# Input projection: sums of squares as rows of four heads side by side, then short products to columns

## The chip, the cores and the metric

The kernel runs on one core of a Trainium2 chip. The metric is the device time of one launch in microseconds (us), taken as the median of several runs; less is better. Here TensorE (PE) multiplies matrices out of SBUF into PSUM, VectorE (DVE) and ScalarE (ACT) do elementwise work and empty PSUM, GpSimd (POOL) and SyncE (SP) carry the rest and the DMA queues. The engines run side by side and meet only at semaphores: an engine that waits on one holds up everything queued behind the wait.

## The reference, cut to what matters

One inference step of two layers over 640 tokens (512 latent, 128 context) of width 1024. Each layer projects its normed input once to all that its three attention branches need. The branch that this change touches is the gated delta net: queries and keys (four heads of 128 features each) go through a short convolution and SiLU, and are then divided by their own length, token by token and head by head:

```python
qkv = _short_conv(dn_qkv, lp['dn_conv_w'])          # 3 taps, then silu
def _l2norm(x):
    xf = x.astype(jnp.float32)
    return xf * lax.rsqrt(jnp.sum(xf * xf, axis=-1, keepdims=True) + EPS)
qn = _l2norm(q) * (DN_DK ** -0.5)
kn = _l2norm(k)
```

So a sum of 128 squares is wanted for each of 640 tokens, 4 heads, and keys and queries: 8 vectors of 640 sums in each of 2 layers.

## The kernel before

**Layout.** Activations lie feature-major: 128 features on the partitions, tokens in the columns. A token's sum of squares is therefore a sum over partitions, which TensorE makes.

**The projection.** `wstat` makes one output tile of 128 features x 640 tokens in PSUM banks 0 to 3 (two banks for each of two tiles in turn). It runs over 8 blocks k of the inner dimension; at each k it issues six matmuls (three products of split numbers, two halves of 320 tokens), 48 in a tile. `for j in range(PT_)` with PT_ = 24 runs 24 such tiles in each layer. Tile 0 holds gates, tiles 1 to 4 the keys (i = 0 to 3), tiles 5 to 8 the queries (i = 4 to 7), tiles 9 to 12 the values, later tiles the inputs of the other branches.

**The other engines** have their own loops over j, each one step behind. At step j DVE (`scaled(j - 1)`, L1737 and L1738) empties tile j-1, at even j splits the next weights (`split_lo`, L1505, after ACT's `split_hi`, L952), and runs the convolution of tile j-2 (`taps`, L1786 and L1789); ACT at step j casts weights (even j), writes tile j-1 out with its bias (`tile_out`, L1154, and the middle tap L1159), and makes SiLU and squares of an earlier tile (`conv_silu(j - 3)`, L1165 and L1170 into `SQT`). In layer 0 alone DVE also makes modulation rows (`mod_tile`, L1765) at steps 2 to 12, and PE, at j = 1 to 9, small products (`ada`, L469, and `adt`, L476) that wait for DVE's copy `ada_row` (L1778) of the previous one.

**The sums of squares.** After tile j (j = 4 to 11) PE waits for the squares of i = j - 4 and multiplies five blocks of 128 tokens of `SQT` (as the stationary operand) by one column of ones (L2442), which gives 5 columns of bank 7. ACT takes roots of the keys' twenty columns at j = 8 (L1197) and of the queries' twenty at j = 12 (L1205); DVE inverts them (L1878, L1833). Eight times a layer PE then spreads a head's inverse lengths over partitions into the bank pair 4 and 5, `pair(2)` (L2462; j = 8 to 11 keys, 13 to 16 queries), and DVE multiplies the head by them (`unit`, L1799, at its steps 9 to 12 and 14 to 17). `unit` counts `chat` up by two. From j = 9 to 12 PE also multiplies unit keys with themselves (L2452, `kdm`), which waits for `chat`.

**After the projection** PE turns values and keys by token and goes on to attention, the delta net's solves, the output projection and the MLP.

Of the kernel before, what the change touches and what calls it, by code (L numbers as in the profile page):

```python
# [7 lines left out]
F32 = mybir.dt.float32  # L8
# [5 lines left out]
P = 128  # L14
# [10 lines left out]
H = 4  # L25
# [82 lines left out]
def rotations():  # L108
# [15 lines left out]
PER = dict(  # L124
    w_mm=TILES, w_ev=TILES, par_in=32, tab_in=16 * 7, s0_in=32, st=64, std=32,
    h_hi=2 * KT, h_lo=2 * KT, h_sh=2, h_sl=2,
    pads=3, p_out=PT_, tap=12, taps=12, conv=12, silu=12, csq=8, css=8, crt=2, crr=2, kdm=4, kde=4, kdw=272, gce=2, gcr=144, mke=1, mex=1, wi=2, leaf=1, wst=320, crb=8, chat=16,
    msq=3, mss=1, mrt=2, mrr=1, mrb=2, map_=3, vtr=4, vte=4, ktr=4, kte=4,
    g_tr=1, g_cp=1, gate_e=2, gate_b=4, gate_mm=1, gate_t=3, gate_x=6,
    ga=96, gb=64, dtm=10, dta=10, eg=8, de=10, dtn=10, ke=8, qe=8, qs=8, kk=9, cm=10, atm=10, u1=20, pm=10, pe_=10,  # L130
# [19 lines left out]
def build(nc, t):  # L150

    ctx = ExitStack()
    with ctx:
# [41 lines left out]
        TSV = place("TSV", [P, T], F32, r_t + 25600)  # L195
        TGK = place("TGK", [P, T], F32, r_t + 28160)
        FLO = place("FLO", [P, H, T], F32R, r_t + 10240)
        SQT = [place(f"SQT{i}", [P, 641], F32, r_t + 10240 + i * 2592) for i in range(2)]
        UUD = [place(f"UUD{d}", [P, H, NB, LEAF], F32, r_t + (17920, 28160)[d]) for d in range(2)]
        UTD = [place(f"UTD{d}", [P, H, NB, LEAF], F32, r_raw + KT * CH * 4 + d * NM * LEAF * 4) for d in range(2)]  # L200
        KDR = place("KDR", [P, LEAF, LEAF], F32, r_x)
# [113 lines left out]
        def bank(i):  # L315
            return PS[:, i, :]
# [42 lines left out]
        def toks(b):  # L359
            return slice(b * P, (b + 1) * P)  # L360
# [12 lines left out]
        def conv_at(i):  # L373

            return (i + 4) % 8 if i < 8 else i
# [123 lines left out]
        with nc.Block() as block:  # L499
# [447 lines left out]
            def _(act):  # L947
# [188 lines left out]
                for l in range(DEPTH):  # L1136
# [25 lines left out]
                    def conv_silu(i):  # L1162

                        act.wait_ge(S["conv"], o["conv"] + i + 1)
                        nc.scalar.activation(QKV[:, conv_at(i), 1:642], TC[i % 2][:, 0:641], ACT.Silu).then_inc(S["silu"], 1)  # L1165
                        if i < 8:
                            act.wait_ge(S["silu"], o["silu"] + i + 1)
                            if i >= 2:
                                act.wait_ge(S["css"], o["css"] + i - 1)
                            nc.scalar.activation(SQT[i % 2][:, :], QKV[:, conv_at(i), 1:642], ACT.Square).then_inc(S["csq"], 1)  # L1170


                    for j in range(PT_ + 1):
# [6 lines left out]
                        if j == 1:  # L1180
                            root(2 * l)
                        if j == CKV0 + 1:
                            act.wait_ge(S["css"], o["css"] + 8)
                        if j == Z0 + 1 and l == 0:
                            act.wait_ge(S["ada_mm"], 8)
                        if j >= 1:
                            tile_out(j - 1)
                        if l == 0 and j == 1:
                            act.wait_ge(vb_in, 16)
                            nc.scalar.activation(CBX[:, :, :], CBX[:, :, :], ACT.Silu).then_inc(silu_c, 1)  # L1190
                        if 0 <= j - 3 < 12:
                            conv_silu(j - 3)
                        if j == 8:
                            act.wait_ge(S["css"], o["css"] + 4)
                            act.wait_ge(S["gce"], o["gce"] + 2)
                            act.wait_ge(S["gate_t"], o["gate_t"] + 2)
                            nc.scalar.activation(SMALL[:, 7, 0:20], bank(7)[:, 464:484], ACT.Sqrt, bias=eps).then_inc(S["crt"], 1)  # L1197
                        if 10 <= j <= 13:
                            h = j - 10
                            act.wait_ge(S["kdm"], o["kdm"] + h + 1)  # L1200
                            nc.scalar.copy(KD[:, h * NB:(h + 1) * NB, :],
                                           bank(7)[:, 208:368].rearrange("p (b c) -> p b c", b=NB)).then_inc(S["kde"], 1)
                        if j == 12:
                            act.wait_ge(S["css"], o["css"] + 8)
                            nc.scalar.activation(SMALL[:, 7, 20:40], bank(7)[:, 484:504], ACT.Sqrt, bias=peps,  # L1205
                                                 scale=float(P)).then_inc(S["crt"], 1)
                        if j == 14:
                            act.wait_ge(S["mke"], o["mke"] + 1)
                            nc.scalar.activation(LM[leafs, :, :, :], LM[leafs, :, :, :], ACT.Exp).then_inc(S["mex"], 1)
# [281 lines left out]
            def _(dve):  # L1491
# [278 lines left out]
                for l in range(DEPTH):  # L1770
# [40 lines left out]
                    for j in range(PT_ + 1):  # L1811
# [17 lines left out]
                        if 9 <= j <= 12:  # L1829
                            unit(j - 9)  # L1830
                        if j == 13:
                            dve.wait_ge(S["crt"], o["crt"] + 2)
# [33 lines left out]
                        if j == 8:  # L1866
                            dve.wait_ge(S["gate_mm"], o["gate_mm"] + 1)
                            for x in (0, 32):
                                nc.vector.tensor_copy(GCT[x:x + NM, :, :],
                                                      bank(7)[x:x + NM, 208:464].rearrange("p (d c) -> p d c", d=2)  # L1870
                                                      ).then_inc(S["gce"], 1)
                            nc.vector.tensor_copy(R[3], bank(7)[:, 128:168]).then_inc(S["gate_t"], 1)
                            nc.vector.tensor_copy(R[4], bank(7)[:, 168:208]).then_inc(S["gate_t"], 1)
                            dve.wait_ge(S["gate_t"], o["gate_t"] + 2)
                            link(nc.vector.tensor_scalar(R[8], R[3], -1.0, None, ALU.mult))
                            nc.vector.tensor_tensor(R[12], R[4], R[3], ALU.subtract).then_inc(S["gate_t"], 1)
                            dve.wait_ge(S["crt"], o["crt"] + 1)
# [407 lines left out]
            @block.tensor  # L2285
            def _(pe):

                def wstat(tile, g, mh, ml, n, lo, c, norm=None, tail=None, ks=range(KT)):

                    s, u = g % 2, tile % 2  # L2290
                    if u == 0:
                        pe.wait_ge(lo_ready, g + 1)
                    if tile >= 2:
                        pe.wait_ge(S["w_ev"], tile - 1)
                    for k in ks:
                        pe.wait_ge(lo, c + k + 1)
                        if k == 5 and norm is not None:
                            norm_turn(norm)
                        cols = slice(k * CH + u * P, k * CH + (u + 1) * P)
                        mlk = tail[:, k - H, :] if tail is not None and k >= H else ml[:, k, :]  # L2300
# [98 lines left out]
                for l in range(DEPTH):  # L2399
# [9 lines left out]
                    def adt(j):  # L2409

                        pe.wait_ge(S["ada_ev"], j + 1)
                        ada_turn(pe, MODB[j % 2], j).then_inc(S["ada_tr"], 1)

                    pe.wait_ge(S["h_sl"], 2 * l + 1)
                    for j in range(PT_):
                        wstat(t0 + j, g0 + j // 2, HH, HL, W1, S["h_lo"], 16 * l, 2 * l if j == 1 else None)
                        if j == 0:
                            norm_sums(2 * l)
                        if j == 3:
# [7 lines left out]
                        if j == 8:  # L2427
                            pe.wait_ge(S["gate_t"], o["gate_t"] + 2)
                            pe.wait_ge(S["gce"], o["gce"] + 2)
                            pe.wait_ge(S["crt"], o["crt"] + 1)  # L2430
                        if 10 <= j <= 13:
                            pe.wait_ge(S["kde"], o["kde"] + j - 9)
                        if j == 12:
                            pe.wait_ge(S["crt"], o["crt"] + 2)
                        if l == 0 and 2 <= j <= 9:
                            adt(j - 2)
                        if 4 <= j <= 11:
                            i = j - 4
                            pe.wait_ge(S["csq"], o["csq"] + i + 1)
                            for b in range(NB):  # L2440
                                c = cblk(b)
                                last = pe.matmul(bank(7)[:, 464 + i * NB + b:465 + i * NB + b],  # L2442
                                                 SQT[i % 2][:, c.start - 1:c.stop - 1], one, start=True, stop=True)
                            last.then_inc(S["css"], 1)
                        if 9 <= j <= 12:
                            h = j - 9
                            pe.wait_ge(S["chat"], o["chat"] + 2 * h + 2)
                            for b in range(NB):
                                for q in range(NQ):
# [558 lines left out]
```

## Time and profile before

| | before |
|---|---|
| median of 3 runs | 1824.38 us (1823.56 to 1825.29) |
| the profiled execution | 1822.96 us, of which the span from first to last instruction is 1821.2 us |
| PE busy | 1745.0 us (96%) |
| DVE busy | 1266.6 us (70%) |
| ACT busy | 847.3 us (47%) |
| mean granted TensorE clock | 0.983 of full |

The page gives busy times, 40 slices of the span with the granted clock, the chain of work that ended last followed back from the end, and the costliest groups of instructions. In all rows, times are us from the start of the span. A float32 matmul stands as two records, so 5 matmuls are x10. The name in front of an arrow is the tile written, the names behind it are those read.

### The profile page before, as it was taken

How to read it: one execution, taken by the hardware profiler on the slowest of the kernel's cores; microseconds unless marked ns; L12 is line 12 of the kernel's file. 1: busy time of each engine (PE TensorE's matmuls, PEld its weight loads, DVE VectorE, ACT ScalarE, POOL GpSimd, SP SyncE). 2: the span in 40 equal slices, each digit the busy share in tenths (PEclk: the TensorE clock that was granted, in tenths of full speed). 3: DMA queues.
4: the chain of work that ended last, by engine and by line, in shares of the span. 5: the costliest groups of instructions: out<-in, count | busy, mean ns of one | idle time of the engine just before them, and what ended most of it. 6: DMA issues, size and time to landing. Idle time of an engine off the chain costs nothing.

```text
span 1821.2 us, 33568 instructions
## 1 busy us (share of the span) xinstructions
PE 1745.0 (96%) x13554; PEld 1658.5 (91%) x13554; DVE 1266.6 (70%) x2117; ACT 847.3 (47%) x1469; POOL 523.9 (29%) x418
## 2 busy tenths in 40 slices
PE   5999999999999999999999999998999999999997
PEld 2889986788999999999999999777899999989997
DVE  2687775687735677676764557666977777788886
ACT  1555426744242231322325653475446666666664
POOL 5000002085442150321551000213832233232225
PEclk9999999989999999999999999998999999999998
DMA  8653223022467879688527761541132777877662
GB/s 344 252 207 93 78 73 68 1 66 88 165 226 218 282 234 325 244 268 275 193 91 204 181 154 47 139 94 42 49 107 85 222 234 249 298 277 256 214 221 91
DMA packets 128037, 316.66 MB, mean 174 GB/s; under 512 B 37828, under 2 KB 64236, under 8 KB 108172
## 3 DMA queue, kind: packets, MB, share of 16 engines
q1 hardware_dynamic: 121740, 279.49, 43.7%
q0 software_dynamic: 4608, 33.56, 9.5%
q8 instruction: 108, 1.77, 0.4%
q10 hardware_dynamic: 1536, 1.48, 0.2%
q14 instruction: 45, 0.37, 0.1%
HBM read 286.01 MB, written 95.49 MB: 209 GB/s over the span
## 4 chain that ended last, share of the span: by engine, by line
PE 82%; DVE 8%; issue 3%; DMA 3%; ACT 3%; SPq 1%; POOL 0%; POOLq 0%; ACTq 0%; DVEq 0%
PE PS L2305 47%; PE PS L2374 18%; PE PS L2668 1%; DMA ADA<-ada 1%; PE PS L2579 1%; PE PS L2757 1%; PE PS L2774 1%; PE PS L2628 1%; PE PS L2607 1%; PE PS L2596 1%; PE PS L2744 1%; DVE WHL L1559 1%; DVE MPR L1765 1%; PE PS L2442 1%; PE PS L2616 1%
## 5 line engine op out<-in xcount | busy, mean ns | idle before, releaser
L2305 PE MATMUL PS<-HH,HI 128*128 128x320 f32 (+1 forms) x1280 | 300.5, 316 | 5.2 <-DVE HL L1514 5.2
L2305 PE MATMUL PS<-HL,HI 128*128 128x320 f32 (+1 forms) x1280 | 295.9, 313 | 0.0
L2305 PE MATMUL PS<-HH,LO 128*128 128x320 f32 (+1 forms) x1280 | 294.5, 311 | 0.0
L952 ACT CAST HI<-RAW 128x2048 fp32r<-128x2048 f32 x64 | 121.9, 1905 | 276.6 <-PE PS L2305 249.4
L2305 PEld LDWEIGHTS PS<-HH,HI 128*128 128x128 f32 x1280 | 216.1, 191 | 5.8 <-issue 5.7
L2305 PEld LDWEIGHTS PS<-HL,HI 128*128 128x128 f32 x1280 | 219.7, 192 | 0.0
L2305 PEld LDWEIGHTS PS<-HH,LO 128*128 128x128 f32 x1280 | 217.7, 191 | 0.0
L2374 PE MATMUL PS<-FB,WHL 128*128 128x320 f32 x1344 | 199.6, 309 | 5.9 <-DVE TMP L1642 3.0
L2374 PEld LDWEIGHTS PS<-FB,WHL 128*128 128x128 f32 x1344 | 197.1, 188 | 8.2 <-DVE WHL L1559 6.2
L2374 PE MATMUL PS<-HB,WHL 128*128 128x322 f32 (+1 forms) x1344 | 200.0, 311 | 3.5 <-issue 1.6
L2374 PEld LDWEIGHTS PS<-HB,WHL 128*128 128x128 f32 x1344 | 199.0, 189 | 4.2 <-issue 2.5
L999 ACT CAST WHL<-RAWB 128x512 fp32r<-128x512 f32 x224 | 137.7, 619 | 111.9 <-PE PS L2374 93.1
L1505 DVE TENSOR_TENSOR LO<-RAW,HI 128x2048 fp32r<-128x2048 f32 x62 | 149.0, 2403 | 57.7 <-ACT HI L952 57.4
L2305 PE MATMUL PS<-FH,HI 128*128 128x320 f32 x768 | 175.5, 310 | 1.6 <-issue 1.6
L1559 DVE TENSOR_TENSOR WHL<-RAWB,WHL 128x512 fp32r<-128x512 f32 x224 | 168.9, 779 | 10.2 <-ACT WHL L999 8.6
L2305 PE MATMUL PS<-FH,LO 128*128 128x320 f32 x768 | 174.6, 308 | 0.0
L1765 DVE SCALAR_TENSOR_TENSOR MPR<-WM,CB 128x1024 f32<-128x1024 f32 x96 | 137.9, 1436 | 12.5 <-DMA WM<-adt 10.9
L2305 PE MATMUL PS<-FL,HI 128*128 128x320 f32 x640 | 145.9, 309 | 0.0
L2305 PEld LDWEIGHTS PS<-FH,HI 128*128 128x128 f32 x768 | 127.8, 188 | 2.0 <-issue 1.1
L2305 PEld LDWEIGHTS PS<-FH,LO 128*128 128x128 f32 x768 | 128.4, 188 | 0.0
L2305 PEld LDWEIGHTS PS<-FL,HI 128*128 128x128 f32 x640 | 107.0, 188 | 0.0
L928 POOL TENSOR_TENSOR TC<-TC 128x640 f32<-128x640 f32 x32 | 50.4, 1575 | 181.4 <-ACT FH L1450 181.4
(355 smaller groups left out, 2909.8 us busy)
## 6 DMA issues: line engine op xcount, KB each, us to landing
RAW<-ws SPq DMA_DIRECT2D x64, 1024.0 KB, 5.0
wp<-ws SPq DMA_DIRECT2D x32, 1024.0 KB, 7.9
RAWB<-wp SPq DMA_DIRECT2D x128, 256.0 KB, 3.9
WM<-adt SPq DMA_DIRECT2D x48, 512.0 KB, 9.1
RAWB<-ws SPq DMA_DIRECT2D x96, 256.0 KB, 3.7
FS<-hb SPq DMA_DIRECT2D x28, 640.0 KB, 7.9
ADA<-ada SPq DMA_DIRECT2D x16, 1024.0 KB, 7.6
wp<-ws POOLq DMA_DIRECT2D x16, 1024.0 KB, 10.2
```

The lines of the kernel that those rows point to most:

```text
L928: nc.gpsimd.tensor_tensor(TC[u][:, 0:T], TC[u][:, 0:T], TC[u][:, 0:T], ALU.mult).then_inc(S["f1_sq"], 1)
L952: nc.scalar.copy(HI[g % 2][:, :], RAW[g % 2][:, :]).then_inc(hi_ready, 1)
L999: nc.scalar.copy(WHL[:, w % SLOTS, 0, :], operand(w)).then_inc(F["whi"], 1)
L1505: last = nc.vector.tensor_tensor(LO[g % 2][:, c], RAW[g % 2][:, c], HI[g % 2][:, c].bitcast(F32), ALU.subtract)
L1559: nc.vector.tensor_tensor(WHL[:, w % SLOTS, 1, :], operand(w), WHL[:, w % SLOTS, 0, :].bitcast(F32), ALU.subtract).then_inc(F["wlo"], 1)
L1765: return nc.vector.scalar_tensor_tensor(out=MPR[:, :], in0=w[:, :], scalar=1.0, in1=cond[:, g, :], op0=ALU.mult, op1=ALU.mult, accum_out=M ...
L2305: last = pe.matmul(bank(2 * u + a)[:, 0:e], w[:, cols], m[:, a * HT:a * HT + e], start=(k == 0 and f), stop=(k == KT - 1 and e_))
L2374: last = pe.matmul(out, x[:, cols], B[:, y, k, 0:n], start=(opens and k == 0 and v == 0), stop=(k == H - 1 and v == 2), skip_group_check=n ...
L2442: last = pe.matmul(bank(7)[:, 464 + i * NB + b:465 + i * NB + b], SQT[i % 2][:, c.start - 1:c.stop - 1], one, start=True, stop=True)
L2579: pe.matmul(pair(0)[:, 0:LAT], q, kt[:, 0:LAT], start=True, stop=True)
L2596: last = pe.matmul(bank(7 if i else 2)[:, c:c + hi - lo], TSQ[rows, p, toks(b)], KSW[rows, lo:hi], start=True, stop=True)
L2607: last = pe.transpose(pair(2)[:, toks(i)], TC[a % 2][:, toks(slot)], ident)
```

## The change

PE no longer makes eight groups of five one-column products a layer. Keys and queries are taken four heads at a time. `square_rows(n)` (n = 0 keys, 1 queries) multiplies 32 columns of ones (stationary) by the squares of a head (moving, 512 and then 128 tokens), for four heads into partitions 0, 32, 64 and 96 of `pair(2)`. ACT copies the 128 x 640 result to a new tile `SQR`. `square_sums(n)` then multiplies the five token blocks of `SQR` (stationary) by four columns of the identity, which puts the same twenty sums into bank 7. `square_rows(0)` stands inside tile 7, before its block k = 2, and `square_rows(1)` at the same place of tile 12; `square_sums` follow after tiles 7 and 12. `SQT` has four buffers where it had two. The queries' root on ACT moves from step 12 to 13.

```diff
-        SQT = [place(f"SQT{i}", [P, 641], F32, r_t + 10240 + i * 2592) for i in range(2)]
+        SQT = [place(f"SQT{i}", [P, 641], F32, r_t + 8192 + i * 2592) for i in range(H)]
+        SQR = place("SQR", [P, T], F32, r_t + 24576)
...
-                            if i >= 2:
-                                act.wait_ge(S["css"], o["css"] + i - 1)
+                            if i >= H:
+                                act.wait_ge(S["css"], o["css"] + 1)
...
                         if j >= 1:
                             tile_out(j - 1)
+                        if j in (7, 12):
+                            act.wait_ge(S["css"], o["css"] + (1 if j == 7 else 3))
+                            nc.scalar.copy(SQR[:, :], pair(2)).then_inc(S["crt"], 1)
...
+                        if j == 13:
+                            act.wait_ge(S["css"], o["css"] + 4)
+                            nc.scalar.activation(SMALL[:, 7, 20:40], bank(7)[:, 484:504], ACT.Sqrt, bias=peps,
+                                                 scale=float(P)).then_inc(S["crt"], 1)
...
-                        if j == 12:
-                            act.wait_ge(S["css"], o["css"] + 8)
-                            nc.scalar.activation(SMALL[:, 7, 20:40], bank(7)[:, 484:504], ACT.Sqrt, bias=peps,
-                                                 scale=float(P)).then_inc(S["crt"], 1)
...
+                        if k == 2 and between is not None:
+                            between()
...
+                    def square_rows(n):
+                        pe.wait_ge(S["csq"], o["csq"] + 4 * n + 4)
+                        if n:
+                            pe.wait_ge(S["chat"], o["chat"] + 8)
+                        else:
+                            pe.wait_ge(S["g_cp"], o["g_cp"] + 1)
+                        for src, dst in ((slice(0, LAT), slice(0, LAT)), (slice(C_CTX - 1, C_CTX - 1 + CTX), slice(LAT, T))):
+                            for i in range(H):
+                                last = pe.matmul(pair(2)[32 * i:32 * i + 32, dst], ones[:, 0:32], SQT[i][:, src],
+                                                 start=True, stop=True)
+                        last.then_inc(S["css"], 1)
+
+                    def square_sums(n):
+                        pe.wait_ge(S["crt"], o["crt"] + 2 * n + 1)
+                        for b in range(NB):
+                            c = 464 + 20 * n + b
+                            last = pe.matmul(bank(7)[:, c:c + 3 * NB + 1:NB], SQR[:, toks(b)], ident[:, 0:P:32],
+                                             start=True, stop=True)
+                        last.then_inc(S["css"], 1)
...
-                        wstat(t0 + j, g0 + j // 2, HH, HL, W1, S["h_lo"], 16 * l, 2 * l if j == 1 else None)
+                        wstat(t0 + j, g0 + j // 2, HH, HL, W1, S["h_lo"], 16 * l, 2 * l if j == 1 else None,
+                              between=(lambda: square_rows(j // 12)) if j in (7, 12) else None)
...
-                        if 4 <= j <= 11:
-                            i = j - 4
-                            pe.wait_ge(S["csq"], o["csq"] + i + 1)
-                            for b in range(NB):
-                                c = cblk(b)
-                                last = pe.matmul(bank(7)[:, 464 + i * NB + b:465 + i * NB + b],
-                                                 SQT[i % 2][:, c.start - 1:c.stop - 1], one, start=True, stop=True)
-                            last.then_inc(S["css"], 1)
+                        if j == 7:
+                            square_sums(0)
...
+                        if j == 12:
+                            square_sums(1)
```

The other hunks raise the counts that PE and DVE wait for by what ACT now signals more (`crt` 2 and 4 in place of 1 and 2), and `css` counts four in place of eight a layer.

## Rows read from the trace of the kernel before

**Rows 1.** The page: busy times, and the chain that ended last, by engine.

```profile
PE 1745.0 (96%) x13554; PEld 1658.5 (91%) x13554; DVE 1266.6 (70%) x2117; ACT 847.3 (47%) x1469; POOL 523.9 (29%) x418
...
PE 82%; DVE 8%; issue 3%; DMA 3%; ACT 3%; SPq 1%; POOL 0%; POOLq 0%; ACTq 0%; DVEq 0%
```

**Rows 2.** The instructions of L2442: durations min/median/max, first and last start.

```profile
L2442 PE MATMUL PS<-K,SQT x160: 165/250/251, 92.5 to 1057.8; 128*128 128x1 f32 x160
```

**Rows 3.** Timeline of PE, layer 0, after tiles 9, 11 and 12.

```profile
145.67 0.50 PE L476 MATMUL PS<-K,MODB 128*128 128x2 f32 x4
...
164.64 1.17 PE L2442 MATMUL PS<-K,SQT 128*128 128x1 f32 x10
165.74 0.56 PE L2452 MATMUL PS<-QKV 128*32 128x32 f32 x40
...
166.75 0.55 PE L2305 MATMUL PS<-HH,HI 128*128 128x320 f32 x2
...
174.02 0.56 PE L2452 MATMUL PS<-QKV 128*32 128x32 f32 x40
```

**Rows 4.** Timeline of PE, layer 1, after tile 11.

```profile
1056.92 1.17 PE L2442 MATMUL PS<-K,SQT 128*128 128x1 f32 x10
1058.02 0.56 PE L2452 MATMUL PS<-QKV 128*32 128x32 f32 x40
...
1059.03 0.55 PE L2305 MATMUL PS<-HH,HI 128*128 128x320 f32 x2
```

**Rows 5.** Timeline of PE, layer 0, after tile 4 (start, duration, instruction).

```profile
91.07 1.07 PE L469 MATMUL PS<-ADA,SC 128*32 128x256 f32 x16
92.07 0.61 PE L476 MATMUL PS<-K,MODB 128*128 128x2 f32 x4
```

**Rows 6.** Chain that ended last: three whole tiles of 48 matmuls.

```profile
222.64 8.71 PE PS L2305 x48
231.90 7.07 PE PS L2305 x48
...
1115.74 9.50 PE PS L2305 x48
```

**Rows 7.** Timeline of PE, layer 0, around the end of tile 7.

```profile
121.21 1.07 PE L469 MATMUL PS<-ADA,SC 128*32 128x256 f32 x16 [0.59 <-DVE MODB L1778]
```

**Rows 8.** Timeline of DVE, layer 0, steps 10 to 12.

```profile
145.94 0.16 DVE L1737 COPY BI<-PS 128x2 f32<-128x2 f32 x1 [1.27 <-PE PS L2305]
...
162.10 0.88 DVE L1799 TENSOR_TENSOR QKV<-QKV,PS 128x512 f32<-128x512 f32 x2
...
165.31 0.15 DVE L1737 COPY BI<-PS 128x2 f32<-128x2 f32 x1
...
166.77 2.29 DVE L1505 TENSOR_TENSOR LO<-RAW,HI 128x2048 fp32r<-128x2048 f32 x1 [0.57 <-ACT HI L952]
...
170.70 0.88 DVE L1799 TENSOR_TENSOR QKV<-QKV,PS 128x512 f32<-128x512 f32 x2
```

**Rows 9.** Chain that ended last: one float32 product of 512 columns, whole array.

```profile
278.86 0.86 PE PS L2534 x2
```

**Rows 10.** ACT's copies of a 128 x 640 pair of banks to SBUF.

```profile
L971 ACT COPY RB<-PS x3: 693/693/693, 60.2 to 971.4; 128x640 f32<-128x640 f32 x3
```

**Rows 11.** Timeline of DVE and ACT, layer 1, step 12.

```profile
1062.98 0.88 DVE L1799 TENSOR_TENSOR QKV<-QKV,PS 128x512 f32<-128x512 f32 x2
...
1057.12 1.90 ACT L952 CAST HI<-RAW 128x2048 fp32r<-128x2048 f32 x1 [5.58 <-PE PS L2305]
```

**Rows 12.** Stretches: us, busy time of PE, PEld, DVE, ACT, POOL, clock, DMA share, GB/s.

```profile
219.40:222.70 3.30, 3.30 (x31) 3.30 (x31) 1.01 (x3) 2.20 (x3) 0.00 (x0) 1.00 0.44 186
222.70:226.40 3.70, 3.70 (x16) 3.70 (x16) 3.00 (x6) 0.52 (x3) 0.00 (x0) 0.54 0.02 4
...
1111.70:1115.70 4.00, 4.00 (x30) 4.00 (x30) 0.89 (x2) 2.30 (x3) 0.00 (x0) 0.77 0.36 152
...
1020.30:1022.80 2.50, 2.50 (x26) 2.25 (x25) 1.35 (x3) 2.38 (x2) 0.00 (x0) 1.00 1.01 210
```

More of the change, by code:

```diff
@@ L126 @@
     h_hi=2 * KT, h_lo=2 * KT, h_sh=2, h_sl=2,
-    pads=3, p_out=PT_, tap=12, taps=12, conv=12, silu=12, csq=8, css=8, crt=2, crr=2, kdm=4, kde=4, kdw=272, gce=2, gcr=144, mke=1, mex=1, wi=2, leaf=1, wst=320, crb=8, chat=16,
+    pads=3, p_out=PT_, tap=12, taps=12, conv=12, silu=12, csq=8, css=4, crt=4, crr=2, kdm=4, kde=4, kdw=272, gce=2, gcr=144, mke=1, mex=1, wi=2, leaf=1, wst=320, crb=8, chat=16,
     msq=3, mss=1, mrt=2, mrr=1, mrb=2, map_=3, vtr=4, vte=4, ktr=4, kte=4,
@@ L1167, in conv_silu @@
                             act.wait_ge(S["silu"], o["silu"] + i + 1)
-                            if i >= 2:
-                                act.wait_ge(S["css"], o["css"] + i - 1)
-                            nc.scalar.activation(SQT[i % 2][:, :], QKV[:, conv_at(i), 1:642], ACT.Square).then_inc(S["csq"], 1)
+                            if i >= H:
+                                act.wait_ge(S["css"], o["css"] + 1)
+                            nc.scalar.activation(SQT[i % H][:, :], QKV[:, conv_at(i), 1:642], ACT.Square).then_inc(S["csq"], 1)
                     for j in range(PT_ + 1):
@@ L1182, in _ @@
                         if j == CKV0 + 1:
-                            act.wait_ge(S["css"], o["css"] + 8)
+                            act.wait_ge(S["css"], o["css"] + 3)
                         if j == Z0 + 1 and l == 0:
@@ L1193, in _ @@
                         if j == 8:
-                            act.wait_ge(S["css"], o["css"] + 4)
+                            act.wait_ge(S["css"], o["css"] + 2)
                             act.wait_ge(S["gce"], o["gce"] + 2)
@@ L1202, in _ @@
                                            bank(7)[:, 208:368].rearrange("p (b c) -> p b c", b=NB)).then_inc(S["kde"], 1)
-                        if j == 12:
-                            act.wait_ge(S["css"], o["css"] + 8)
-                            nc.scalar.activation(SMALL[:, 7, 20:40], bank(7)[:, 484:504], ACT.Sqrt, bias=peps,
-                                                 scale=float(P)).then_inc(S["crt"], 1)
                         if j == 14:
@@ L1831, in _ @@
                         if j == 13:
-                            dve.wait_ge(S["crt"], o["crt"] + 2)
+                            dve.wait_ge(S["crt"], o["crt"] + 4)
                             nc.vector.reciprocal(SMALL[:, 7, 20:40], SMALL[:, 7, 20:40]).then_inc(S["crr"], 1)
@@ L1876, in _ @@
                             nc.vector.tensor_tensor(R[12], R[4], R[3], ALU.subtract).then_inc(S["gate_t"], 1)
-                            dve.wait_ge(S["crt"], o["crt"] + 1)
+                            dve.wait_ge(S["crt"], o["crt"] + 2)
                             nc.vector.reciprocal(SMALL[:, 7, 0:20], SMALL[:, 7, 0:20]).then_inc(S["crr"], 1)
@@ L2286, in _, with wstat @@
             def _(pe):
-                def wstat(tile, g, mh, ml, n, lo, c, norm=None, tail=None, ks=range(KT)):
+                def wstat(tile, g, mh, ml, n, lo, c, norm=None, tail=None, ks=range(KT), between=None):
                     s, u = g % 2, tile % 2
@@ L2429, in _ @@
                             pe.wait_ge(S["gce"], o["gce"] + 2)
-                            pe.wait_ge(S["crt"], o["crt"] + 1)
+                            pe.wait_ge(S["crt"], o["crt"] + 2)
                         if 10 <= j <= 13:
                             pe.wait_ge(S["kde"], o["kde"] + j - 9)
-                        if j == 12:
-                            pe.wait_ge(S["crt"], o["crt"] + 2)
+                        if j == 13:
+                            pe.wait_ge(S["crt"], o["crt"] + 4)
                         if l == 0 and 2 <= j <= 9:
                             adt(j - 2)
-                        if 4 <= j <= 11:
-                            i = j - 4
-                            pe.wait_ge(S["csq"], o["csq"] + i + 1)
-                            for b in range(NB):
-                                c = cblk(b)
-                                last = pe.matmul(bank(7)[:, 464 + i * NB + b:465 + i * NB + b],
-                                                 SQT[i % 2][:, c.start - 1:c.stop - 1], one, start=True, stop=True)
-                            last.then_inc(S["css"], 1)
+                        if j == 7:
+                            square_sums(0)
                         if 9 <= j <= 12:
```

## The prediction

> **What bounds the kernel now.** I read the page first: PE is busy for 96% of the span and carries 82% of the chain that ended last [rows 1]. So work taken from PE counts in full wherever PE is what ends last, and only there. The next view is the timeline of PE in the projection. After each of tiles 4 to 11 stands one group of L2442 [rows 2]: it starts at 164.64 and what follows it at 165.74 [rows 3], 1056.92 and 1058.02 in layer 1 [rows 4]. A group holds PE for 1.10 us. A plain tile takes 7.07 us [rows 6], 0.885 us for one of its 8 blocks k.
>
> The third view is DVE's, for the reader must know who is late where. In layer 0 DVE carries the modulation rows on top, and up to tile 7 PE waits for it: the product at 121.21 had been held 0.59 us by DVE's copy [rows 7]. At steps 11 and 12 DVE is late too: it empties tile 11 at 165.31, though PE was through with it at 164.64 [rows 3, 8]. In layer 1 DVE keeps up.
>
> **Work of PE.** Removed: 16 groups x 1.10 = 17.6 us. Added: four `square_sums`, each five products with a 128-column stationary block, like L2442 but with four moving columns in place of one: 4 x 1.10 = 4.4 us. Added: four `square_rows`. The trace has their very form in L469: 32 stationary columns, results in four groups of partitions, 16 records for two rounds of 256 columns. It starts at 91.07 and what follows at 92.07 [rows 5]: 1.00 us for 512 columns, four products side by side, so 1.25 us for 640. If they ran one after another, a whole product of 512 columns at 0.86 us [rows 9] would give 4 x 0.86 x 640/512 = 4.3 us. The range of the price is 1.25 to 4.3; I take 1.25, since L469 has the same shape. Four cost 5.0 us. PE's work falls by 17.6 - 4.4 - 5.0 = 8.2 us.
>
> Here a rule of the Trainium skill speaks against the change: the page TensorEngine Tiling (Array Packing), section Instruction Overhead, gives a matmul an overhead of some 60 cycles, so that one column costs what 60 do. By that, an estimate from its figure at 2.4 GHz is 25 ns a record and 0.25 us a group, 12 groups fewer would save 3 us and the rows cost 5. The measured 1.10 us for ten records contradicts it, and by the row the exchange is good work for PE.
>
> **ACT.** Four copies of 128 x 640 are added, 0.69 us each [rows 10], and no work is removed. At step 7 ACT first waits for tile 6 anyway, and `square_rows(0)` comes 1.8 us into tile 7; ACT's copy has the other six blocks, 5.3 us, before `square_sums(0)` asks for it. It is hidden; without that cover it would cost 0.7 us. The queries' root moves one step later: DVE meets it about 0.6 us late, PE needs its result only a tile (7 us) later. I count nothing, with 0 to 0.6 us as bounds.
>
> **The new wait, and it is the main term.** `square_rows(1)` overwrites `pair(2)`, from which DVE still multiplies the last key head. So PE waits for `chat` 8, DVE's `unit` of step 12, and now inside tile 12, before block k = 2. Before, the wait for the same count stood after tile 12, where it cost nothing. Behind it are queued six blocks of tile 12 and all later PE work; DVE's emptying of tile 12 and ACT's writing wait for those.
>
> Layer 1: the unit of step 12 ends at 1062.98 + 0.88 = 1063.86, 6.94 us after tile 11's end at 1056.92 [rows 4, 11]. That distance follows PE: ACT's cast starts at tile 11's end (1057.12), then come DVE's split, taps and unit. PE's own work from tile 11's end to block 2 is short: products and spread, 1059.03 - 1058.02 = 1.01 us [rows 4], and two blocks, 1.77 us, together 2.78. So PE stands for 6.94 - 2.78 = 4.16 us. Balance of layer 1: seven groups gone (tiles 4 to 6 and 8 to 11) -7.7, one replaced by its equal after tile 7, rows twice +2.5, `square_sums(1)` +1.1, wait +4.16: +0.1 us, nothing.
>
> Layer 0: what PE gains after tiles 4 to 6 (3.3 us) is given back at 121.21, where it waits longer for DVE; the rows of tile 7 (1.25) fit into that wait. From there: the group after tile 8 falls away, tile 9 ends at 145.67 - 1.10 = 144.57. DVE, idle 1.27 us before 145.94, can start step 10 at 144.67 at the earliest, so it moves by about 1.10 us, and no more, however early PE is. The unit of step 11 then ends at 162.10 + 0.88 - 1.10 = 161.88 and holds PE's products after tile 11 (which ends at 164.64 - 3 x 1.10 = 161.3). PE reaches block 2 of tile 12 at 161.88 + 1.01 + 1.77 = 164.66. DVE's step 12 moves by the same 1.10 and by the 0.57 us that its split waited for ACT: the unit ends at 170.70 + 0.88 - 1.67 = 169.91 [rows 8]. PE stands for 5.25 us. Tile 12 then ends at 169.91 + 1.25 + 6 x 0.885 = 176.47, where it ended at 174.02 [rows 3]: 2.4 us late, and 3.5 with `square_sums(1)`. After step 12 PE is the bound again (its tiles follow each other in the chain), so 3.5 us stay.
>
> Both layers: +3.5 + 0.1 = +3.6 us, less work and yet a longer way.
>
> **The clock.** Two stretches of this trace show what a thin PE does to its clock. From 222.70 the granted clock was 0.54 (of its two levels, 2.4 and 1.2 GHz, nearly all the lower), after 3.3 us of one-column products at the full clock, and the tile there took 8.71 in place of 7.07 us, +1.64; in layer 1 the clock fell within 4.0 such us already (0.77) and the tile took 9.50, +2.43. After 2.5 thin us at 1020.3 the clock stayed at 1.00 [rows 6, 12]. Each new wait, 5.25 and 4.16 us with nothing, followed by 1.25 us of narrow rows, is thinner than the stretches that lost the clock. The bounds are 0 (the loss falls into the wait itself) and 2.43 each. I take 1.6 each, the nearer row, since part of the slow time may lie in the wait: +3.2 us. The page TensorE: Matmul & The Clock Gate of the Trainium skill (Part 1) says that 1.2 GHz is the clock of an idle engine and that sustained work releases 2.4 GHz; the rows agree, with 0.54 of full there.
>
> Sum: +3.6 + 3.2 = +6.8 us. The profiled execution took 1822.96 us (span 1821.2 and 1.8 around it); it would take 1829.8. Against the median of the runs, 1824.38, which is 1.4 above the profiled one, I put 1831.2.
>
> **Rivals.**
> First, the clock holds through both waits: +3.6 us, 1828.0; with one loss, 1829.6. For it: no row shows a bare wait of this length in the middle of the kernel, only thin work. Against it: thin work of 3.3 us lost the clock in both layers.
>
> Second, the faster side: the wait hardly binds, since DVE comes to `unit` earlier once PE and ACT leave it more room, and the work saved shows. Wholly unbound, and with layer 0's gain kept, it is -8.2 us, 1816.2. It decides at waits that sum to under 9.4 - 3.6 = 5.8 us with the clock kept. Against it: cast, split, taps and units form a chain of 6.94 us that starts only when tile 11 ends, and DVE stands in it without a gap worth the name.
>
> Third, the rows don't run side by side: 3.05 us more each time, hidden in part in layer 0's tile 7, so about +9.2 on top, 1840. Against it is L469.
>
> That the change doesn't do what it says would show as L2442 at its old count; the diff leaves no room for that.
>
> **How the numbers follow.** Both waits, at least one with a lost clock: 0.68 (1829.6 to 1834, likeliest 1831.2). Both waits and the clock kept: 0.14, at 1828.0, right at the edge that I call a difference. Waits small, faster: 0.10; in between, within 0.2%: 0.03. Rows one after another: 0.05. A measurement of this kernel can tell about 0.2%, 3.6 us. Slower by more: 0.68 + 0.05 + a small part of 0.14 = 0.75; within: 0.15; faster: 0.10. The range goes from 1827.0 to 1834.5: it takes in the kept clock and two losses of 2.4 us, and leaves out 0.10 below and under 0.10 above.
>
> **What the profile would show.** Right: PE idle for 4 to 5 us before the rows in tile 12 of both layers, released by DVE's L1799; the rows as 16 records in 1.25 us; the group starting at 121.21 in layer 0 not moved; stretches at half clock behind both waits; the later tiles of layer 0 about 3.5 us late, before the clock. Wrong: no idle time there, or a tile 7 of layer 0 that ends its group earlier, which would mean that DVE was not the bound.

## The result

Over 22 runs of each, in turn on one chip, the kernel before took 1822.70 us (median, 1819.55 to 1826.14) and the changed kernel 1826.51 us (1823.53 to 1830.43): 1.0022 times as long, with a 95% interval of 1.0015 to 1.0028. The change costs 3.8 us (2.7 to 5.1), although PE has less work. A second set of 10 runs on another occasion gave 1827.19 against 1821.68 us, 1.0030 (1.0019 to 1.0040). The forecast was 1831.2 us with a range from 1827.0: the direction and the new wait came true, the size did not, and the time lies just below the range.

The profiled execution of the changed kernel took 1827.66 us. The page of the changed kernel, beside [rows 1]:

```profile
PE 1736.1 (95%) x13498; PEld 1644.0 (90%) x13498; DVE 1268.3 (69%) x2117; ACT 850.1 (47%) x1473; POOL 525.5 (29%) x418
...
PE 80%; DVE 11%; issue 4%; ACT 3%; DMA 2%; SPq 0%; ACTq 0%; POOL 0%; POOLq 0%; DVEq 0%
```

PE has 8.9 us less to do (1745.0 to 1736.1; 8.2 were worked out). In the chain that ended last PE's share has fallen from 82 to 80% and DVE's has risen from 8 to 11%. What stands behind it is a line in the view of PE's waits, changed kernel (total, times, longest):

```profile
PE PS L2429 <- DVE QKV L1803: 8.9, 2, 4.9
```

L2429 makes the new rows, L1803 multiplies a key head by its inverse lengths. The timeline of PE in the changed kernel, layer 0, from the end of tile 7 to the start of tile 13:

```profile
121.77 1.07 PE L470 MATMUL PS<-ADA,SC 128*32 128x256 f32 x16 [1.40 <-DVE MODB L1782]
...
134.49 1.07 PE L470 MATMUL PS<-ADA,SC 128*32 128x256 f32 x16
...
162.27 0.54 PE L2311 MATMUL PS<-HH,HI 128*128 128x320 f32 x2
169.20 2.11 PE L2429 MATMUL PS<-SQT,K 128*32 128x512 f32 x16 [4.91 <-DVE QKV L1803]
171.24 0.90 PE L2311 MATMUL PS<-HH,HI 128*128 128x320 f32 x2
...
177.50 0.56 PE L2475 MATMUL PS<-QKV 128*32 128x32 f32 x40
177.99 1.28 PE L2438 MATMUL PS<-K,SQR 128*128 128x4 f32 x10
179.13 0.53 PE L2311 MATMUL PS<-HH,HI 128*128 128x320 f32 x2
```

and in layer 1, from tile 12's rows to tile 13:

```profile
1060.47 2.36 PE L2429 MATMUL PS<-SQT,K 128*32 128x512 f32 x16 [4.00 <-DVE QKV L1803]
1062.77 0.90 PE L2311 MATMUL PS<-HH,HI 128*128 128x320 f32 x2
...
1068.71 0.56 PE L2475 MATMUL PS<-QKV 128*32 128x32 f32 x40
1070.34 0.53 PE L2311 MATMUL PS<-HH,HI 128*128 128x320 f32 x2
```

The waits are 4.91 and 4.00 us (5.25 and 4.16 were worked out). The rows behind them take 2.04 us (169.20 to 171.24) and 2.30 us, though in tile 7, at the full clock, they take 1.23. The chain that ended last, changed kernel, layer 0, shows what PE waits through: DVE empties tile 11, splits weights, runs the taps and only then the unit.

```profile
163.61 0.73 DVE TMP L1742
164.34 2.20 DVE LO L1509
166.54 0.81 DVE TC L1790
...
168.18 0.89 DVE QKV L1803 x2
169.06 0.14 issue
169.20 2.11 PE PS L2429 x16
```

**Two marks.** A single span scatters by 3 us, so the experiments are also read by two distances in each trace, called marks here. Layer 0: from the product after tile 7 to the start of tile 13. Layer 1: from the start of tile 4 to the start of tile 13. In the kernel before, the ends of these distances that no row has shown yet are

```profile
174.52 0.56 PE L2305 MATMUL PS<-HH,HI 128*128 128x320 f32 x2
...
988.49 0.56 PE L2305 MATMUL PS<-HH,HI 128*128 128x320 f32 x2
...
1066.80 0.56 PE L2305 MATMUL PS<-HH,HI 128*128 128x320 f32 x2
```

so 174.52 - 121.21 [rows 7] = 53.31 us and 78.31 us. In the changed kernel, where tile 4 of layer 1 starts at 989.87, they are 57.36 us (+4.05) and 80.47 us (+2.16).

### The profile page after: what moved, and what is told of

Read it like the earlier page. It is cut to its first block, busy times and chain, and to the rows that moved or that the text cites. A ratio compares the mean times of both kernels' runs of the same rounds, so it can differ in the third digit from the quotient of the medians.

```text
span 1825.9 us, 33462 instructions
## 1 busy us (share of the span) xinstructions
PE 1736.1 (95%) x13498; PEld 1644.0 (90%) x13498; DVE 1268.3 (69%) x2117; ACT 850.1 (47%) x1473; POOL 525.5 (29%) x418
## 3 DMA queue, kind: packets, MB, share of 16 engines
q8 instruction: 108, 1.77, 0.4%
## 4 chain that ended last, share of the span: by engine, by line
PE 80%; DVE 11%; issue 4%; ACT 3%; DMA 2%; SPq 0%; ACTq 0%; POOL 0%; POOLq 0%; DVEq 0%
PE PS L2311 46%; PE PS L2380 19%; DMA ADA<-ada 2%; PE PS L2604 1%; DVE MPR L1769 1%; PE PS L2653 1%; PE PS L2632 1%; PE PS L2621 1%; DVE LO L1509 1%; PE PS L2693 1%; PE PS L2769 1%; PE PS L2799 1%; PE PS L2555 1%; PE PS L2641 1%; PE PS L2782 1%
## 5 line engine op out<-in xcount | busy, mean ns | idle before, releaser
L1741 DVE COPY BI<-PS 128x2 f32<-128x2 f32 x80 | 12.6, 158 | 132.0 <-PE PS L2311 119.7
```

## The experiments

Theory 1 is that of the prediction: the queries' rows, moved into tile 12, make PE wait for DVE's last unit key, the wait costs its length, and the clock lost behind it costs more. Theory 2: the new work itself costs more than its time, since narrow products break into a dense tile or ACT's copies delay others. A third question is layer 0, where the keys' half should bring nothing, as DVE is the bound there; its rival is that PE's work counts in both layers. Each row of the table has one trace and 6 to 22 runs.

All numbers "against before" are medians of the runs of one session, with the ratio and its 95% interval.

| kernel | against before, us | ratio (interval) | layer 0, us | layer 1, us |
|---|---|---|---|---|
| before | | | 53.31 | 78.31 |
| changed | +3.8 | 1.0022 (1.0015 to 1.0028) | 57.36 | 80.47 |
| changed, second set | +5.5 | 1.0030 (1.0019 to 1.0040) | 57.37 | 80.49 |
| other banks | -4.4 | 0.9971 (0.9960 to 0.9982) | 50.76 | 74.87 |
| other banks, second set | -6.7 | 0.9967 (0.9955 to 0.9979) | 52.14 | 74.92 |
| before the last block | -5.4 | 0.9969 (0.9957 to 0.9981) | 51.96 | 75.55 |
| before the fifth block | +2.4 | 1.0016 (1.0004 to 1.0027) | 55.63 | 77.20 |
| wait filled with work | +4.7 | 1.0021 (1.0010 to 1.0032) | 55.67 | 78.89 |
| keys alone | -2.0 | 0.9984 (0.9973 to 0.9996) | 53.35 | 76.45 |
| queries alone | +8.6 | 1.0042 (1.0029 to 1.0055) | 57.73 | 83.49 |

**The changed kernel once more.**

> The changed kernel once more, beside the others on one chip. It was 1826.51 us against 1822.70 before, +3.8. Every theory expects +2.5 to +5 again; the runs below are read against this one. In the trace: waits of PE of 4.9 us (layer 0) and 4.0 us (layer 1) ahead of the rows in tile 12, and half clock behind one or both.

+5.5 us. The two marks are those of the first trace to 0.02 us: where the kernel is late, it is late in both traces alike.

**Other banks: the wait taken away.**

```diff
                         if n:
-                            pe.wait_ge(S["chat"], o["chat"] + 8)
+                            if l == 0:
+                                pe.wait_ge(S["ada_ev"], 8)
...
-                                last = pe.matmul(pair(2)[32 * i:32 * i + 32, dst], ones[:, 0:32], SQT[i][:, src],
+                                out = pair(2) if n == 0 else bank(6) if dst.start == 0 else bank(7)
+                                if n and dst.start:
+                                    dst = slice(32, 32 + CTX)
+                                last = pe.matmul(out[32 * i:32 * i + 32, dst], ones[:, 0:32], SQT[i][:, src],
...
-                            nc.scalar.copy(SQR[:, :], pair(2)).then_inc(S["crt"], 1)
+                            if j == 7:
+                                nc.scalar.copy(SQR[:, :], pair(2)).then_inc(S["crt"], 1)
+                            else:
+                                nc.scalar.copy(SQR[:, 0:LAT], bank(6))
+                                nc.scalar.copy(SQR[:, LAT:T], bank(7)[:, 32:32 + CTX]).then_inc(S["crt"], 1)
```

> The rows of the queries go to bank 6 and to free columns of bank 7 instead of the bank pair that DVE still reads; place in tile 12 unchanged, the wait for the last unit key is gone, the copy is made in two pieces. Theory 1 (the wait and the clock lost behind it are the cost): tile 13 starts 6.9 us earlier in layer 0 and 5.9 us earlier in layer 1 than in the changed kernel; against before -6 to -9 us, about 1815.5. Theory 2 (products of 32 columns between the blocks of a tile cost more than their 1.25 us, or ACT's copies delay DVE): +2 to +4 as now, since place, rows and copies remain.

-4.4 us, faster than both kernels, and again in a second set:

> The kernel with the rows of the queries in other banks once more: a second figure for the one that beats both. Local gains in its trace were 2.55 us in layer 0 and 3.44 us in layer 1, 6.0 in all; -4 to -6 us against before.

-6.7 us there (ratio 0.9967). The timeline of PE, first set, layer 0:

```profile
164.10 1.30 PE L2437 MATMUL PS<-SQT,K 128*32 128x512 f32 x16
165.32 0.56 PE L2315 MATMUL PS<-HH,HI 128*128 128x320 f32 x2
...
172.44 0.53 PE L2315 MATMUL PS<-HH,HI 128*128 128x320 f32 x2
```

The same rows at the same place take 1.22 us, nothing precedes them, and tile 13 starts 6.6 us (layer 0 mark) and 5.6 us (layer 1) earlier than in the changed kernel, where 6.9 and 5.9 were expected. Theory 2 falls: narrow products inside a tile and ACT's copies cost little more than their own time. In layer 1 the groups taken away and the rows and sums put in are 3.85 us less work of PE by the rows of the two traces, and the mark fell by 3.44, so that 0.4 us is left for it there. The wait, with what hangs on it, is the whole loss.

**Before the last block, and before the fifth.** One line each: `k == 2` becomes, for tile 12, `k == 7` and `k == 4`.

> The rows of the queries stand before the last block of tile 12 (k = 7) instead of the third; all else as in the changed kernel. Theory 1: PE arrives there 4.4 us later, about when the unit key is done: a wait of 0.6 us left in layer 0 and none in layer 1, no half clock, tile 13 starts 6.3 and 5.9 us earlier; against before -6 to -8 us, about 1816. Rival: the next thing is late in its place (ACT's copy to the row tile ahead of the short products, or the root that DVE and PE want a tile later), so that 1 to 3 us of it come back as a wait after tile 12: -3 to -5 us.

-5.4 us. The timeline of PE, layer 0:

```profile
169.45 1.29 PE L2429 MATMUL PS<-SQT,K 128*32 128x512 f32 x16 [0.49 <-DVE QKV L1803]
...
172.36 0.56 PE L2475 MATMUL PS<-QKV 128*32 128x32 f32 x40 [0.54 <-ACT KD L1209]
```

0.49 us of the wait are left, as worked out (0.6). What is late in its place is ACT, which stands in its queue for the rows and so copies the key products late: 0.54 us here and 0.55 in layer 1. Tile 13 starts 5.4 us (layer 0) and 4.9 us (layer 1) earlier than in the changed kernel, where 6.3 and 5.9 were expected. So the rival's thing that is late next exists, and costs 1.1 us by these waits. The time lies between the two ranges, -6 to -8 and -3 to -5.

"No half clock" did not come true either. Tile 13 of layer 1, which starts at the end of the mark, takes 8.71 us (1060.88 to 1069.59) where it took 7.14 in the changed kernel. The stretch, in the columns of [rows 12]:

```profile
1060.80:1064.40 3.60, 3.60 (x15) 3.60 (x16) 2.32 (x4) 3.18 (x5) 0.00 (x0) 0.53 0.89 169
```

Ahead of it PE had the rows, one block, the key products with their wait of 0.55 us and the short sums; no wait was longer. A long wait is therefore not the only thing in front of which the half clock stands.

> The rows of the queries stand before block k = 4 of tile 12 instead of k = 2, that is 2 x 0.885 = 1.77 us later. The wait falls from 4.9 to 3.1 us in layer 0 and from 4.0 to 2.2 us in layer 1, whatever the clock does. If the clock is lost only behind the longer waits, tile 13 starts 3.5 us earlier in each layer than in the changed kernel, -7 us in all, and the kernel ends some 2 us below the one before. If it is lost as before, -3.5 us in all, and the kernel ends about where the one before does, +1 us.

+2.4 us. PE waits 3.16 us in layer 0 and 2.20 in layer 1:

```profile
168.76 2.26 PE L2429 MATMUL PS<-SQT,K 128*32 128x512 f32 x16 [3.16 <-DVE QKV L1803]
...
1056.88 1.28 PE L2429 MATMUL PS<-SQT,K 128*32 128x512 f32 x16 [2.20 <-DVE QKV L1803]
```

Behind the longer wait the rows take nearly twice their time (2.19 us to the next block), behind the shorter one they don't (1.22). Layer 0 gains 1.73 us against the changed kernel (the 1.77 us of shorter wait and no more), layer 1 gains 3.27 us, nearly twice that. So in the traces with rows in tile 12 the clock was lost behind each wait of 3.16 to 4.94 us and kept behind the one of 2.20. By the marks the kernel is 1.2 us slower than the one before; it is 2.4 (0.7 to 4.9).

**The wait filled with work: what the clock alone costs.**

```diff
                         if n:
+                            for r in range(24):
+                                pe.matmul(bank(6)[:, 0:HT], HI[0][:, 0:P], HH[:, 0, 0:HT], start=True, stop=True)
                             pe.wait_ge(S["chat"], o["chat"] + 8)
```

> Ahead of the wait in tile 12 stand 24 more products of the tile's own form into bank 6, which nothing reads: 24 x 0.148 = 3.5 us of work inside waits of 4.9 and 4.0 us. Theory 1, with the clock as a term of its own: the waits shrink to 1.4 and 0.5 us, the rows start when they did, the half clock behind them is gone, and tile 13 starts 1.75 and 1.7 us earlier: -3.4 us against the changed kernel, about +0.4 against before. Rival (the clock lost here costs nothing in the mean, since the low time would fall elsewhere): within 1 us of the changed kernel.

+4.7 us. The timeline of PE with the filled wait, layer 0 (these products are of the tile's form and stand as one record each, x24):

```profile
164.68 3.68 PE L2425 MATMUL PS<-HH,HI 128*128 128x320 f32 x24
169.66 1.29 PE L2431 MATMUL PS<-SQT,K 128*32 128x512 f32 x16 [1.30 <-DVE QKV L1803]
170.88 0.56 PE L2311 MATMUL PS<-HH,HI 128*128 128x320 f32 x2
...
178.00 0.55 PE L2311 MATMUL PS<-HH,HI 128*128 128x320 f32 x2
```

The stretches behind the waits, first of the changed kernel, then of the filled one (us, busy time of PE, PEld, DVE, ACT, POOL, granted clock, DMA share, GB/s):

```profile
169.00:172.50 3.50, 3.30 (x21) 1.99 (x22) 2.43 (x5) 1.15 (x2) 0.89 (x1) 0.57 0.51 213
1060.00:1063.90 3.90, 3.42 (x20) 1.82 (x21) 0.33 (x2) 1.00 (x2) 0.00 (x0) 0.56 1.03 296
```

```profile
169.00:172.50 3.50, 2.84 (x27) 2.04 (x28) 2.98 (x6) 1.48 (x3) 0.33 (x1) 1.00 0.63 260
1060.00:1063.90 3.90, 3.53 (x32) 2.47 (x31) 0.66 (x2) 1.51 (x3) 0.64 (x1) 1.00 0.99 330
```

More work at the same end of the wait gives 1.00 in place of 0.57 and 0.56, and the marks fall by 1.69 and 1.58 us (57.36 to 55.67, 80.47 to 78.89). That is the clock's price where it is lost; 1.6 was taken. The times say less: 1826.42 us against 1827.19 for the changed kernel on the same chip, 0.8 us where 3.4 were expected, with intervals that overlap. So locally theory 1 holds to 0.1 us. For the whole kernel the number is the rival's, by which the low time would fall elsewhere (within 1 us of the changed kernel); with these intervals the pair alone doesn't settle it.

**Keys alone, queries alone.** One half of the change each; the other four heads keep their one-column groups after tiles 8 to 11 or 4 to 7. From keys alone:

```diff
-                              between=(lambda: square_rows(j // 12)) if j in (7, 12) else None)
+                              between=(lambda: square_rows(j // 12)) if j == 7 else None)
...
-                        if j == 12:
-                            square_sums(1)
+                        if 8 <= j <= 11:
+                            i = j - 4
+                            pe.wait_ge(S["csq"], o["csq"] + i + 1)
...
```

> The change for the four key heads alone; the queries' sums are one-column products after tiles 8 to 11 again, and there is no new wait. By my reckoning the 3.3 us saved after tiles 4 to 6 of layer 0 are given back to DVE: the product at 121.21 stays within 0.2 us (apart from what the prologue shifts), and tile 13 of layer 0 starts where it did in the kernel before. Layer 1 gains 3 x 1.10 - 1.23 = 2.1 us. Sum -2 us. Rival, that PE's work counts in both layers: -4.1 us, with the product at 121.21 2 us earlier.

-2.0 us. The product after tile 7, timeline of PE, keys alone:

```profile
120.94 1.07 PE L470 MATMUL PS<-ADA,SC 128*32 128x256 f32 x16 [1.40 <-DVE MODB L1782]
```

It stands where it stood (121.21), only PE's idle time before it has grown from 0.59 to 1.40 us. The mark of layer 0 moves by 0.04 us, that of layer 1 by -1.86 (expected 0 and -2.1).

> The change for the four query heads alone, with its wait in tile 12; keys as before. By my reckoning layer 0 is as in the changed kernel (waits and clock included, tile 13 about 4 us late, apart from the prologue), since the keys' half brought nothing there, and layer 1 is 2.1 us worse than in the changed kernel, +4.2: in all 2 us above the changed kernel, +6 to +8 against before. Rival, that PE's work counts in both layers: 4.1 us above the changed kernel, +8 to +10.

+8.6 us, 3.1 or 4.8 us more than the whole change (+5.5, +3.8), where 2 were expected and the rival had 4.1: with these intervals the time alone doesn't decide. The marks do: layer 0 stands at 57.73, within 0.4 us of where the changed kernel has it, and layer 1 is 3.0 us worse (83.49 against 80.47; 2.1 expected). 1.2 us of the 3.0 is the clock: the six blocks behind the rows took 7.12 us (1064.35 to 1071.47) where they took 5.94 in the changed kernel (1062.77 to 1068.71). So one lost clock cost 1.6 us there and 2.8 here. All the harm is in the queries' half.

**Layer 0 without DVE's rows.** Both kernels with `mod_tile` cut to 8 columns in layer 0, which leaves that part of the computation out, so that only the times mean something:

```diff
-                        return nc.vector.scalar_tensor_tensor(out=MPR[:, :], in0=w[:, :], scalar=1.0, in1=cond[:, g, :],
+                        few = slice(0, 8 if n < MF else D)
+                        return nc.vector.scalar_tensor_tensor(out=MPR[:, few], in0=w[:, few], scalar=1.0, in1=cond[:, g, few],
```

> The kernel before, with the modulation rows that DVE makes in layer 0 beside the projection cut to 8 of 1024 columns (this part of the computation is left out; their number and their semaphores stay). DVE is then no longer late in layer 0. Expected: PE's waits for DVE's copies at tiles 1 to 7 are gone (some 2.7 us of idle time in layer 0), the low clock at 124 us may move; tile 13 of layer 0 starts 2 to 4 us earlier than in the kernel before.

> The changed kernel with the same part left out. If DVE's load is what swallowed the keys' gain in layer 0, then against the same cut of the kernel before the products after tile 7 of layer 0 now start 3.3 - 1.2 = 2.1 us earlier, the wait in tile 12 is 4.2 us as in layer 1, not 4.9, and tile 13 starts about 2 us late (0.1 and the clock) where it started 4 late with the rows. If the keys' gain went elsewhere (the rows inside the tile, the copy), these products stay where they were and the delay is still 4 us.

Before, cut: 1819.91 against 1821.56 us (0.9990, 0.9978 to 1.0002). Changed, cut: 1822.92 us (1.0003, 0.9993 to 1.0014). In the timelines the product after tile 7 starts at 120.54 in the first and 117.92 in the second, 2.6 us earlier, where with DVE's rows it had not moved:

```profile
117.92 1.07 PE L470 MATMUL PS<-ADA,SC 128*32 128x256 f32 x16
...
162.13 2.36 PE L2430 MATMUL PS<-SQT,K 128*32 128x512 f32 x16 [4.00 <-DVE QKV L1804]
...
171.86 0.53 PE L2312 MATMUL PS<-HH,HI 128*128 128x320 f32 x2
```

The wait is 4.00 us, that of layer 1. Tile 13 starts at 171.86 against 170.80, 1.1 us late (about 2 expected; it is 4.6 with DVE's rows, 0.56 of it from the prologue). So DVE's load did swallow the keys' gain.

**A plain delay.** Does a delay here reach the end at all? In the kernel before, after tile 13 of layer 0, and in another kernel of layer 1:

```diff
+                        if l == 0 and j == 13:
+                            for r in range(48):
+                                pe.matmul(bank(6)[:, 0:HT], HH[:, 1, 0:P], HH[:, 0, 0:HT], start=True, stop=True)
```

> The kernel before with 48 more products of the tile's form (48 x 0.148 = 7.1 us of PE, result unread) after tile 13 of layer 0: a plain delay of PE at the place where the changed kernel is late, without any lost clock. What arrives at the end tells whether later stages give back a delay of layer 0. If PE is the bound from there on: +7.1 us at the end, and layer 1 starts 7.1 us late. If a later stage waits for others anyway (DVE's small steps, DMA): +5 us or less, with the difference gone before layer 1 starts.

> The same 48 products after tile 13 of layer 1. If PE is the bound from there on: +7.1 us. If layer 1 gives back and layer 0 does not, the local delays of the changed kernel (4.05 and 2.16 us) would have to be weighed by layer.

1829.76 and 1829.59 against 1823.43 us: +6.3 and +6.2 us by the medians, 1.0040 (1.0028 to 1.0053) and 1.0039 (1.0025 to 1.0053) by the ratios, which is 7.3 and 7.1. All or nearly all arrives, from both layers. "+5 or less", which was said of layer 0, falls by a little: the interval there begins at 5.1 us, that of layer 1 at 4.6.

## Why the prediction was right, and where it was wrong

**Work of PE: right.** 8.9 us less by the page, 8.2 worked out. The count of records is exact (160 gone and 104 new, 13554 to 13498); the tenths of the busy time are luck, since the second trace of the changed kernel has 1732.4 us, 3.7 less than the first. The rows run side by side: 1.23 us at the full clock, as L469 had promised with 1.25.

**The groups of layer 0 that bring nothing: right.** Keys alone leaves the layer 0 mark within 0.04 us; cutting DVE's rows brings the gain back.

**The wait: right in place, cause and size.** 4.91 and 4.00 us for 5.25 and 4.16; with other banks it is gone, and that kernel beats the two others.

**The clock: right locally.** Half clock behind both waits; 1.69 and 1.58 us for 1.6. Queries alone shows 2.8 for one of them, beyond my upper bound of 2.43.

**Layer 1: nearly.** I had +0.1 us without the clock; the traces give 2.16 - 1.58 = 0.6. Five of the eight groups held PE for 1.03 us in layer 1 (1003.87 to 1004.90, for one), where I took 1.10 for all; that is 0.3 us. The rest is not traced.

**The balance of layer 0: its parts were not fixed.** I took tile 8 as it stood in the trace of before, with its low clock, and 3.5 us without the new clock loss. The traces give 4.05 - 1.69 = 2.4. The reason is in the stretches of tile 8, kernel before and changed kernel:

```profile
126.00:129.50 3.50, 3.50 (x14) 3.50 (x15) 3.40 (x8) 1.56 (x3) 0.00 (x0) 0.50 0.64 195
129.50:133.00 3.50, 3.50 (x22) 3.50 (x21) 2.15 (x8) 3.21 (x5) 0.00 (x0) 0.81 0.33 140
```

```profile
126.00:129.50 3.50, 3.50 (x17) 3.50 (x17) 3.43 (x6) 2.11 (x3) 0.00 (x0) 0.63 0.61 188
129.50:133.00 3.50, 3.50 (x26) 3.50 (x25) 2.15 (x7) 2.68 (x3) 0.00 (x0) 1.00 0.49 206
```

The low clock was shorter in the changed kernel's trace, so tile 8 ended earlier, ACT's cast was ready when DVE wanted it at step 10, and DVE's chain to the unit lost its wait. DVE's split of step 10, before and changed:

```profile
147.80 2.29 DVE L1505 TENSOR_TENSOR LO<-RAW,HI 128x2048 fp32r<-128x2048 f32 x1 [0.97 <-ACT HI L952]
...
145.95 2.28 DVE L1509 TENSOR_TENSOR LO<-RAW,HI 128x2048 fp32r<-128x2048 f32 x1
```

Nothing in the runs ties this to the change: other banks in its second trace had the long low clock (0.50, then 0.86) and a mark of 52.14, in its first the short one and 50.76; the kernel before with 48 more products in layer 0 (the plain delay above) had the short one and stood at 174.15 - 122.37 = 51.78, not 53.31. Like against like, the changed kernel is 57.36 - 51.78 = 5.6 us late in layer 0, where I had 3.5 + 1.6 = 5.1. With the long low clock on both sides, the unit of step 11 started 160.65 - 120.85 = 39.80 us after the product of tile 7 in other banks' second trace and 162.10 - 121.21 = 40.89 before: 1.09 us earlier, and 1.10 were worked out.

**The step that failed is the last one, the sum: the clock's +3.2 us, added in full to the end time.** By the traces' marks the loss is 4.05 + 2.16 = 6.2 us, or 7.7 with like tiles 8, beside my 6.8. The kernel loses 3.8 (2.7 to 5.1) in one set and 5.5 (3.5 to 7.3) in the other. I had added each clock loss in full, and with it assumed that the rest of the kernel stays as it is. From tile 13 of layer 0 to tile 4 of layer 1 the trace of before took 988.49 - 174.52 = 813.97 us and that of the changed kernel 989.87 - 179.13 = 810.74: 3.2 us of the loss come back where nothing was changed. Part of it is the one trace of before, the longest of all. The other traces say how much is left. This stretch took

- with half clock in tile 12 of layer 0: 810.74 and 809.93 us (changed kernel, twice), 809.90 (queries alone), 809.34 (before the fifth block);
- without it: 811.98 and 810.96 (other banks, twice), 811.34 (before the last block), 812.20 (wait filled), 812.04 (keys alone), 812.11 (delay in layer 1) and 811.3 (delay in layer 0, less the 7.1 us of its 48 products).

The two groups don't overlap, and their medians, 809.9 and 812.0, lie 2.1 us apart. That is about what one lost clock cost at its place. 6.2 less 2.1 is 4.1, and 7.7 less 2.1 is 5.6; the two sets measured 3.8 and 5.5. The filled wait fits: it saves 3.3 us by its marks, 1.5 or 2.3 of them come back in this stretch, and the medians show 0.8. A plain delay was not given back. Against it stands the changed kernel without DVE's rows: its clock was lost too, and it took 812.48 us there, beside 811.61 in its pair. Behind the lost clock of layer 1 no such difference shows, and in the medians of the other kernels it can't be told from the scatter. So the fitting term is the clock's: 1.6 us is what a lost clock costs where it falls, not what it adds to the kernel. How much it adds in the mean, and why the rest of layer 0 is shorter behind it, stays open: it rests on single traces, and no experiment was made on it.

**The start of the count was off too.** My base of 1824.38 us was the median of 3 runs; 22 runs give 1822.70. With my sum on that base I would have said 1829.5; with the measured shift on mine, 1828.2, inside the range.

**The rivals.** The clock holds through both waits (+3.6): the time is near it and the traces contradict it, a right number for a wrong reason. The faster side was to come under waits of 5.8 us in sum with the clock kept: before the fifth block, with 5.4 us and one clock loss, the kernel is still slower by 2.4; before the last block, with 0.5, it is 5.4 faster. Rows one after another: no.

## What to carry to other kernels

Before a product is moved forward in its engine's queue, look at what its output buffer still holds: a wait for the same semaphore count that cost nothing at the end of a tile cost 4 to 5 us a quarter of the way in. Work saved in front of a wait for another engine is not saved; ask which engine the stretch follows, before counting. And a free buffer elsewhere, or a place later in the same tile, was worth 10 to 11 us here against the same work with the wait (1817.26 and 1816.30 against 1827.19).

## What the runs showed of the hardware

A lost clock is not only a cost of its own. In layer 0 the traces with the longer low stretch in tile 8 stand 1.4 to 1.5 us later at a point five tiles on (52.14 against 50.76, 53.31 against 51.78), and DVE's step 10 shows PE's delay arriving through its waits for PE and for ACT's cast. It differs between executions of one kernel. The effect has a limit: in the kernel with its rows before the last block, the granted clock stayed at 1.00 in tile 8, and the products after tile 11 still started 39.50 us after the product of tile 7 (161.53 - 122.03), as in the changed kernel (161.27 - 121.77), since both waited for DVE there.

Of the waits of PE ahead of the rows, 3.16 us was followed by half clock and 2.20 us was not; work in the array during the wait kept the clock, although nobody reads its result. Narrow work with no wait over 0.55 us was followed by half clock too (0.53 in tile 13 of layer 1).
